# The third block's gates of the second token half also through a table in HBM

## The reference, cut to what matters

```python
s = einsum('thpc,hpkc->thpk', q, sub_keys)         # 8 heads, two halves, 128 keys each
sv, si = top_k(s, 16)
cand = sv[:, :, 0, :, None] + sv[:, :, 1, None, :]  # 16 x 16 pairs of keys
best, pos = top_k(cand, 16)
g = softmax(best)                                   # 8 x 16 = 128 picks of a token
act = gelu(einsum('ted,td->te', u_tab[eidx], x))
y = einsum('te,ted->td', g * act, v_tab[eidx])
```

## Time and profile before

| | us |
|---|---|
| three timed runs | 2058.8, 2061.26, 2061.39; median 2061.26 |
| the profiled execution | 2061.06 |
| its span, first to last instruction | 2059.2 |
| PE busy | 2011.5 (98%) |
| DVE busy | 1544.0 (75%) |
| ACT busy | 959.6 (47%) |
| POOL busy | 784.4 (38%) |
| DMA | 387.68 MB, mean 188 GB/s |

### The profile page before, as it was taken

The page is one execution under the profiler, slowest core; times in us unless marked ns, Lnnn a source line. Parts: engine busy times, 40 slices in busy tenths (PEclk is TensorE's granted clock), DMA queues, the critical chain, the costliest instruction groups (busy, mean ns, idle before and its releaser), DMA issues.

```text
span 2059.2 us, 37564 instructions
## 1 busy us (share of the span) xinstructions
PE 2011.5 (98%) x14922; PEld 1852.2 (90%) x14922; DVE 1544.0 (75%) x2886; ACT 959.6 (47%) x1642; POOL 784.4 (38%) x502
## 2 busy tenths in 40 slices
PE   8999999999999999999998999999999999999998
PEld 7899999999889988887897999999998899888886
DVE  7868996555676578878699879975556766679886
ACT  5654453434444444444655654443434434444443
POOL 1014027777730055642110050088787400456420
PEclk9999999999999999999999999999999999999999
DMA  6684556676765568996422444566667655578973
GB/s 224 211 315 152 168 160 152 156 150 151 183 184 163 178 197 271 329 340 222 133 92 69 128 134 153 174 150 149 157 151 171 182 171 177 190 265 295 326 257 102
DMA packets 165918, 387.68 MB, mean 188 GB/s; under 512 B 55920, under 2 KB 78704, under 8 KB 163440
## 3 DMA queue, kind: packets, MB, share of 16 engines
q1 hardware_dynamic: 113712, 332.58, 49.4%
q0 software_dynamic: 49152, 33.75, 10.4%
q10 hardware_dynamic: 2880, 18.96, 2.3%
HBM read 361.67 MB, written 23.54 MB: 187 GB/s over the span
## 4 chain that ended last, share of the span: by engine, by line
PE 81%; DVE 14%; issue 2%; DMA 2%; ACT 2%; SPq 0%; DVEq 0%; ACTq 0%
PE ps L942 15%; PE ps L944 14%; PE ps L943 14%; PE ps L973 11%; PE ps L975 10%; PE ps L974 10%; PE ps L1020 4%; DVE w_lo L1534 2%; DMA land<-stream_dram 2%; DVE work L1420 2%; ACT w_hi L632 1%; DVE hidden L1420 1%; DVE hidden L1555 0%; DVE hidden L1546 0%; DVE work L1428 0%
## 5 line engine op out<-in xcount | busy, mean ns | idle before, releaser
L1534 DVE TENSOR_TENSOR w_lo<-land,w_hi 128x1024 fp32r<-128x1024 f32 x562 | 686.1, 1221 | 357.1 <-ACT w_hi L632 356.0
L942 PE MATMUL ps<-act_hi,w_hi 128*128 128x288 f32 x2688 | 808.6, 301 | 13.6 <-DVE act_lo L1260 4.8
L632 ACT CAST w_hi<-land 128x1024 fp32r<-128x1024 f32 x592 | 621.5, 1050 | 419.6 <-PE ps L975 299.5
L943 PE MATMUL ps<-act_hi,w_lo 128*128 128x288 f32 x2688 | 795.2, 296 | 0.0
L944 PE MATMUL ps<-act_lo,w_hi 128*128 128x288 f32 x2688 | 792.3, 295 | 0.0
L548 POOL DMA_INDIRECT gates_d<-rstd x256 | 452.6, 1768 | 320.1 <-DVE rstd L1687 193.4
L942 PEld LDWEIGHTS ps<-act_hi,w_hi 128*128 128x128 f32 x2688 | 506.0, 188 | 20.1 <-issue 8.9
L944 PEld LDWEIGHTS ps<-act_lo,w_hi 128*128 128x128 f32 x2688 | 508.1, 189 | 0.0
L943 PEld LDWEIGHTS ps<-act_hi,w_lo 128*128 128x128 f32 x2688 | 507.1, 189 | 1.0
L973 PE MATMUL ps<-w_hi,g_hi 128*128 128x512 f32 x1024 | 403.3, 394 | 5.7 <-DVE g_lo L1839 5.7
L974 PE MATMUL ps<-w_lo,g_hi 128*128 128x512 f32 x1024 | 399.7, 390 | 0.0
(11 more groups left out here) (223 smaller groups left out, 1497.0 us busy)
## 6 DMA issues: line engine op xcount, KB each, us to landing
land<-stream_dram SPq DMA_DIRECT2D x592, 512.0 KB
gates_d<-hidden ACTq DMA_DIRECT2D x16, 1024.0 KB, 5.9
work<-gates_d SPq DMA_DIRECT2D x96, 128.0 KB, 4.5
act_d<-smp_stage SPq DMA_DIRECT2D x64, 64.0 KB
gates_d<-rstd POOLq DMA_INDIRECT x256
hidden<-stream_dram,smp_idx POOLq DMA_INDIRECT x128, 5.9
x<-x_dram SPq DMA_DIRECT2D x4, 288.0 KB, 5.2
y_t_dram<-hidden SPq DMA_DIRECT2D x8, 144.0 KB, 1.9
```

Of the source, the lines that this page charges most:

```text
L632: nc.scalar.copy(w_hi[:, m, :], land[:, n % LANDS, :]).then_inc(w_hi_ready, 1)
L942: nc.tensor.matmul(out, w_hi[:, slot, wsl], hi, start=start, stop=False)
L943: nc.tensor.matmul(out, w_lo[:, slot, wsl], hi, start=False, stop=False)
L1534: V.tensor_tensor(w_lo[:, k, :], land[:, n % LANDS, :], w_hi[:, k, :].bitcast(F32), ALU.subtract).then_inc(lo_by_dve, 1)
```

## The change

The gates of tokens 128 to 255 for tiles 96 to 127 no longer go by one-hots: the 8 chunks of block 2 are dropped (`HOT_BLOCKS = 2`), and a second table per layer takes their place. Of it only the tiles from 96 on are zeroed and read: four more zero fills (two a layer, all four in steps 26 to 32 of layer 0), and 16 more loads of a pair a layer, through four buffers of `gate_land[1]` in the part of `work` that the keys use, in steps 260 to 284. All 128 picks of these tokens are added to the table. POOL's order becomes: heads 0 to 3 of the first table; then, four times, a head of the first and a head of the second; heads 4 and 5 of the second; the act fetches; head 6 of the second; and head 7 of the second in pairs of additions between the row fetches of the first samples. The first table's loads begin in step 192 instead of 180. The samples are added in steps 236 to 285 and summed in step 286. The keys of layer 1 are loaded in step 291 instead of 264, behind the last pair of the second table; the conv state stays in step 264 with a semaphore of its own.

```diff
-GCH = [(TP - t0) // t for t, t0 in zip(GTOK, GTOK0)]
+HOT_BLOCKS = 2
+GCH = [(TP - t0) // t if b < HOT_BLOCKS else 0 for b, (t, t0) in enumerate(zip(GTOK, GTOK0))]
...
-APPLY_AT = [BLOCK_START[1] - 20 + 2 * k for k in range(PAIRS)]
+APPLY_AT = [BLOCK_START[1] - 8 + 2 * k for k in range(PAIRS)]
+SUMMED1 = BLOCKS[2][0]
+PAIRS1 = (P - SUMMED1) // 2
+GATE_LANDS1 = 4
+APPLY1_AT = [min(BLOCK_START[2] - 4 + 2 * k, SLABS - 18 + k - (PAIRS1 - TWICE)) for k in range(PAIRS1)]
...
-ZERO_AT = [3 + 2 * z for z in range(DEPTH * ZERO_N)]
+ZERO1_N = (P - SUMMED1) * P // ZERO_W
+ZERO_AT = [3 + 2 * z for z in range(DEPTH * ZERO_N)] + [Q0 + 2 + 2 * z for z in range(DEPTH * ZERO1_N)]
...
-ADD0, ADD1 = BLOCK_START[1] + 26, SLABS - 12
-ADD_AT = [ADD0 + k * (ADD1 - ADD0) // (SMP - 1) for k in range(SMP)]
-SMP_SUM, SMP_OUT = SLABS - 11, SLABS - 9
+MIXED = 8
+ADD0, ADD1, ADD2 = BLOCK_START[1] + 36, BLOCK_START[1] + 53, SLABS - 11
+ADD_AT = [ADD0 + k * (ADD1 - ADD0) // MIXED for k in range(MIXED)]
+ADD_AT += [ADD1 + k * (ADD2 - ADD1) // (SMP - 1 - MIXED) for k in range(SMP - MIXED)]
+SMP_SUM, SMP_OUT = SLABS - 10, SLABS - 8
...
+                if r - 2 in APPLY1_AT:
+                    k = APPLY1_AT.index(r - 2)
+                    if k == 0:
+                        sp.wait_ge(gate_added[1], 16 * PICKS * (L + 1))
+                        sp.wait_ge(gated, GATES * (L + 1))
+                    if k >= GATE_LANDS1:
+                        sp.wait_ge(pair_gated[1], PAIRS1 * L + k - GATE_LANDS1 + 1)
+                    two = slice(SUMMED1 + 2 * k, SUMMED1 + 2 * k + 2)
+                    sp.dma_start(gate_land[1][:, k % GATE_LANDS1, :],
+                                 gates_d[L][1][:, two, :].rearrange("j i t -> j (i t)")
+                                 ).then_inc(gate_landed[1][k % GATE_LANDS1], 16)
...
+            def add_picks(L, u, picked):
+
+                cells = gates_d[L][u].rearrange("j i (t one) -> (j i t) one", one=1)
+                for k in picked:
+                    if k and k % ADDS == 0:
+                        pool.wait_ge(gate_added[u], 16 * (PICKS * L + k))
+                    nc.gpsimd.indirect_dma_start(
+                        out=cells, out_offset=bass.IndirectOffsetOnAxis(ap=add_idx[u][:, k:k + 1], axis=0),
+                        in_=add_val[u][:, k:k + 1], in_offset=None, compute_op=ALU.add).then_inc(gate_added[u], 16)
+
             def add_gates(L):
...
+                def head(u, h):
+                    add_picks(L, u, range(h * ADDS, h * ADDS + ADDS))
+
+                pool.wait_ge(adds_ready, 2 * L + 1)
+                pool.wait_ge(zeroed, 16 * ZEROS)
+                for h in range(4):
+                    head(0, h)
+                pool.wait_ge(adds_ready, 2 * L + 2)
+                for h in range(4):
+                    head(0, h + 4)
+                    head(1, h)
+                head(1, 4)
+                head(1, 5)
...
+                add_picks(L, 1, range(6 * ADDS, 7 * ADDS))
                 rows = stream.rearrange("s p (two w) -> (s p two) w", two=2)
                 for k in range(SMP):
+                    if 0 < k <= MIXED:
+                        first = 7 * ADDS + 2 * (k - 1)
+                        add_picks(L, 1, range(first, first + 2))
...
                         if e >= SUMMED0:
-                            act.wait_ge(pair_gated, PAIRS * L + (e - SUMMED0) // 2 + 1)
+                            act.wait_ge(pair_gated[0], PAIRS * L + (e - SUMMED0) // 2 + 1)
+                        if e >= SUMMED1:
+                            act.wait_ge(pair_gated[1], PAIRS1 * L + (e - SUMMED1) // 2 + 1)
...
                     if r == BLOCK_START[2] and L == 0:
+                        act.dma_start(cstate, cstate_d).then_inc(cstate_in, 16)
+                    if r == SLABS - 5 and L == 0:
+                        act.wait_ge(pair_gated[1], PAIRS1)
                         act.dma_start(keys, keys_d[1]).then_inc(loaded_l, 16)
-                        act.dma_start(cstate, cstate_d).then_inc(loaded_l, 16)
...
                 soften(L, 0)
-                prepare_adds(L)
+                prepare_adds(L, 0)
                 second_level(L, 2, some_lo)
                 soften(L, 1)
+                prepare_adds(L, 1)
                 soften(L, 2)
...
+                    while paired1 < PAIRS1 and APPLY1_AT[paired1] <= r:
+                        apply_pair(L, paired1, 1)
+                        paired1 += 1
```

More of the change, by code:

```diff
@@ L235, in build @@
         tok_row = sb("tok_row", [P, 1])
-        gates_d = [nc.dram_tensor(f"gates_d{i}", (P, P, P), F32).ap() for i in range(DEPTH)]
+        gates_d = [[nc.dram_tensor(f"gates_d{i}_{u}", (P, P, P), F32).ap() for u in range(2)] for i in range(DEPTH)]
         act_d = [nc.dram_tensor(f"act_d{i}", (P, P, TS), F32).ap() for i in range(DEPTH)]
@@ L405, in build @@
         adds_ready = sem("adds_ready")
-        gate_added = sem("gate_added")
-        gate_landed = [sem(f"gate_landed_{k}") for k in range(GATE_LANDS)]
-        pair_gated = sem("pair_gated")
+        gate_added = [sem("gate_added_0"), sem("gate_added_1")]
+        gate_landed = [[sem(f"gate_landed_{u}_{k}") for k in range((GATE_LANDS, GATE_LANDS1)[u])] for u in range(2)]
+        pair_gated = [sem("pair_gated_0"), sem("pair_gated_1")]
+        cstate_in = sem("cstate_in")
         g_hi_ready = sem("g_hi_ready")
@@ L538, in wide_weights @@
                     nc.gpsimd.tensor_copy(wide_w[:, :, t, t:t + CF_W], taps).then_inc(wide_ready, 1)
-            def add_gates(L):
-                pool.wait_ge(adds_ready, L + 1)
-                pool.wait_ge(zeroed, 16 * DEPTH * ZERO_N)
-                cells = gates_d[L].rearrange("j i (t one) -> (j i t) one", one=1)
-                for k in range(PICKS):
-                    if k and k % ADDS == 0:
-                        pool.wait_ge(gate_added, 16 * (PICKS * L + k))
-                    nc.gpsimd.indirect_dma_start(
-                        out=cells, out_offset=bass.IndirectOffsetOnAxis(ap=add_idx[:, k:k + 1], axis=0),
-                        in_=add_val[:, k:k + 1], in_offset=None, compute_op=ALU.add).then_inc(gate_added, 16)
+            def add_picks(L, u, picked):
[6 more added lines that the diff above has]
+                        in_=add_val[u][:, k:k + 1], in_offset=None, compute_op=ALU.add).then_inc(gate_added[u], 16)
+            def add_gates(L):
+                def head(u, h):
[10 more added lines that the diff above has]
+                head(1, 5)
             def fetch_samples(L):
@@ L636, in zero @@
                 if r in ZERO_AT:
-                    L, z = divmod(ZERO_AT.index(r), ZERO_N)
+                    at = ZERO_AT.index(r)
+                    if at < DEPTH * ZERO_N:
+                        u, (L, z) = 0, divmod(at, ZERO_N)
+                    else:
+                        u, (L, z) = 1, divmod(at - DEPTH * ZERO_N, ZERO1_N)
                     act.wait_ge(zeros_ready, 1)
-                    rows = gates_d[L].rearrange("j i t -> j (i t)")
-                    act.dma_start(rows[:, z * ZERO_W:(z + 1) * ZERO_W], zeros).then_inc(zeroed, 16)
+                    rows = gates_d[L][u].rearrange("j i t -> j (i t)")
+                    lo = u * SUMMED1 * P + z * ZERO_W
+                    act.dma_start(rows[:, lo:lo + ZERO_W], zeros).then_inc(zeroed, 16)
             def square(c, x_count):
@@ L1686, in prepare_adds, with apply_pair @@
+                dve.wait_ge(picks_ready, 3 * L + u + 1)
                 settle()
-                V.tensor_copy(add_val, picks_tok[:, 0, 2, :]).then_inc(adds_ready, 1)
-            def apply_pair(L, k):
-                e, buf = SUMMED0 + 2 * k, k % GATE_LANDS
+                V.tensor_copy(val, picks_tok[:, u, 2, :]).then_inc(adds_ready, 1)
+            def apply_pair(L, k, u):
+                lands, pairs = (GATE_LANDS, GATE_LANDS1)[u], (PAIRS, PAIRS1)[u]
+                e, buf = (SUMMED0, SUMMED1)[u] + 2 * k, k % lands
@@ L1692, in apply_pair @@
                 for half in range(2):
                     dve.wait_ge(evacuated[half], L * USES + USE_U + (e + 2) // 2)
-                dve.wait_ge(gate_landed[buf],
-                            16 * (L * len(range(buf, PAIRS, GATE_LANDS)) + k // GATE_LANDS + 1))
-                two = hidden[:, e % HELD:e % HELD + 2, 0:P]
-                V.tensor_tensor(two, gate_land[:, buf, :].rearrange("p (i t) -> p i t", i=2), two,
-                                ALU.mult).then_inc(pair_gated, 1)
+                dve.wait_ge(gate_landed[u][buf], 16 * (L * len(range(buf, pairs, lands)) + k // lands + 1))
@@ L1700, in add_late @@
+                two = hidden[:, e % HELD:e % HELD + 2, u * P:u * P + P]
+                V.tensor_tensor(two, gate_land[u][:, buf, :].rearrange("p (i t) -> p i t", i=2), two,
+                                ALU.mult).then_inc(pair_gated[u], 1)
             def add_late(L, half):
@@ L1863, in peer @@
                 add_late(L, 0)
-                assert made == applied == GATES and paired == PAIRS
```

(1 more changed line is left out.)

39 lines of the change are left out of this document (21 added, 18 removed).

## The result

The change makes the kernel slower: 2189.54 us, median of five runs (2184.26 to 2192.96), beside 2060.19 (five runs) for the kernel before on the same chip, a ratio of 1.0625 with a 95% interval of 1.061 to 1.064. The forecast was 2131 with a range up to 2165: the side was right, and the size was half, 70 us of 129. The profiled execution took 2187.93 us, 126.9 more than that of before, so its trace can be set against the forecast's sum.

A forecast was written before the change was run, and what follows sets the result against it. TensorE, busy 98% of the span, was taken as the bound. Layers at +35.2 and +35.8 us and small terms at -1 made +70 on 2061.06: 2131 us, forecast range 2105 to 2160, 8-in-10 range 2075 to 2165.

The forecast's parts named there:

- step 194: Where SP asks for the first table; forecast complete at 680 us, asked for at 688.68, so no standstill there.
- The saving: On PE, the third block's 8 expansion chunks a layer vanish, 1.22 us each: 9.8 us a layer won.
- Additions up to 708 us at 2.13: On POOL, one addition with its issue gap takes 2.13 us until block 1's last one-hots end, about 708 us.
- Additions behind 708 us at 1.97: On POOL, one addition with gap takes 1.97 us after block 1's one-hots end, an estimate between 1.84 and 2.13.
- The standstill: PE stands ahead of slab 238 while DVE waits for sample 0: 34.0 us in layer 0, 34.6 in layer 1.
- Samples 1 to 7 at 10 a layer: POOL needs 6.9 us per sample, due every 5.44; DVE waits 1.46 for each of seven; bounds 8 and 15.
- DVE's last stretch at 1 a layer, bounds 0 and 4: Second-table pairs and five more samples fill DVE to 77.5 us against 75.3; slabs in hand cover part: 1 us a layer.
- The keys at -5: Moving the key load away from the conv state in layer 0 wins back 5 us; bounds 0 and 6.3.
- The fills at 3: Four more 1 MB zero fills in layer 0, where DVE waits for the last fill: 3 us lost, between 0 and 13.
- the index at 1 a layer: Second index computation on DVE while PE waits for the first one-hots: 2 us for two layers, 0 to 2.5.
- A: Rival: POOL's additions run at their 1.84 us floor and everything is hidden, giving 2040.5 us; chance 0.10.
- B: Rival: additions at 2.4 us make the first table late too, SP stands 21 us at slab 194, 2231 us; chance 0.06.

The follow-up runs named there:

- the run with four heads: The changed kernel without heads 4 to 7 of the second table (half of its additions) in each layer: 2053.38 us, ratio 0.9957 to the kernel before.
- the thin subtraction: The changed kernel with w_lo of the slabs in steps 200 to 238 computed for 8 of 1024 columns only: 2145.93 us, ratio 1.0406 to the kernel before.

## Why the prediction was wrong

The mechanism was right: the late act fetches, DVE waiting for sample 0 ahead of the next g_lo, PE standing in one place of each layer, then seven smaller waits, and no trouble at step 194. Its sizes weren't.

- **The saving**: 9.8 a layer forecast for eight expansions. The seven in slabs 200 to 236 bring 9.3 and 9.4, and the eighth another 1.2 in slab 240. Right, and rather more.
- **Additions up to 708 us at 2.13**: the 96 between 477.95 and 684.16 have a pitch of 2.15. Right.
- **Additions behind 708 us at 1.97**, "about midpoint of 1.84 and 2.13": the step that failed. In the V steps they take 2.21 and with the gap 2.5 to 2.7, more than anywhere. I took the mean's excess over 1.54 for work that grows less when the one-hots end there. Most of it is w_lo, which every slab has; and where a slab holds little that shifts the beat, one addition after the other meets it. The trace of the kernel before has this already: a held addition ends some 1.42 us behind the end of the DVE instruction that it met. Paired so, 38 of the 57 us that its 256 additions take above 1.54 each belong to w_lo and 15 to the one-hots. The row that said so, the most of 2.55 in the earlier trace rows, I set aside as an exception. The last three heads took 117.5 us for some 103: 22 additions up to slab 200 at a pitch of 2.18, then 26 in V steps at 2.68, one wait for a landing in each part.
- **The standstill**: first rows at 874.65 for 854.5, landed 17.6 us later than forecast, of which 6 are covered because the whole layer is 6.5 late; 45.5 us for 34.0. In layer 1 it is 48.0 for 34.6. DVE's wait has two parts, 13.6 us for the acts and 33.2 for the rows, where one of some 35 was forecast.
- **Samples 1 to 7 at 10 a layer**: 13.5 and 15.1 in the table, but the same slabs are 2.2 and 2.6 us shorter than before in the run with four heads, where no sample is late. So the term is 15.7 and 17.7, above the upper end of 15. That the additions make it is shown by the run without head 7.
- **DVE's last stretch at 1 a layer, bounds 0 and 4**: the second failure, 6.9 and 9.5. I summed DVE's busy times over the whole stretch and took every row as landed. DVE's fullness alone costs 4.1 in layer 1 (four heads); without head 7's additions 2.1 and 4.0 are lost. So some 5 us a layer come from head 7's additions. In layer 1 their way is to be seen: DVE waits four times for a sample's rows, 6.0 us in all. The lines behind this list show two of these waits, PE's standstill behind them, and then 7 us with a granted clock of 0.52, so the lower level (1.2 GHz) for nearly all of it. In layer 0 no such wait stands in this stretch, and how head 7 costs 5 us there stays open.
- **The keys at -5**: 3.5 by the trace and 2.5 by the runs, alone; under the late samples nothing of it is to be seen.
- **The fills at 3, the index at 1 a layer**: 6.5 in layer 0 for both, 0.3 in layer 1 for the index, within their bounds.
- **The range** ended at 2165, since no bound held V steps at 2.5 and none held DVE's stretch above 4.

```profile
2081.40 1.28 DVE L1810 SCALAR_TENSOR_TENSOR hidden<-hidden,smp_act 128x1024 f32<-128x1024 f32 x1 [2.81 <-DMA hidden<-stream_dram,smp_idx]
...
2085.24 1.28 DVE L1810 SCALAR_TENSOR_TENSOR hidden<-hidden,smp_act 128x1024 f32<-128x1024 f32 x1 [0.75 <-DMA hidden<-stream_dram,smp_idx]
2086.44 0.69 DVE L1894 TENSOR_TENSOR g_lo<-hidden,g_hi 128x512 fp32r<-128x512 f32 x1
```

```profile
2087.27 0.76 PE L1021 MATMUL ps<-w_hi,g_hi 128*128 128x512 f32 x1 [3.33 <-DVE g_lo L1894]
```

```profile
2086.00:2093.00 7.00, 5.73 (x14) 4.56 (x15) 5.86 (x8) 0.68 (x2) 5.78 (x5) 0.52 0.94 320
```

Of the rivals, A was refuted, though its ground was real: an addition costs 1.54 where DVE leaves it alone. B didn't come, no wait stands at step 194; additions as dear as its own did, but behind step 200. The Trainium skill, "SBUF — State Buffer", section "Who interferes with whom", has two statements that bear on this. One is that, of DVE in a 2-port mode and GpSimd, whichever gets the shared pair of ports first blocks the other for its whole instruction. For this subtraction the trace shows the like: the addition goes on only when the whole w_lo, or the half that it met, has ended (1.55 to 2.42 us, and 1.72 with halves). The other is that `tensor_tensor` doesn't stall descriptor building, given there as inferred. For the indirect additions here the runs say otherwise: the thin subtraction took them back from 2.42 to 1.55.

## What to carry to other kernels

A free engine's idle time must be priced at what its instructions cost beside the work of the very steps in which they will run, and the most in a view is a candidate for the mean there. Look for a beat: an instruction that waits for another engine's periodic one, with a length near the period, falls into step with it. Before moving work off the bound to an engine with slack, count everything that comes behind it on that engine up to its last due date, not only the part that moves.

## What the hardware showed that was not expected

- An indirect DMA that adds 128 gates takes POOL 1.54 us undisturbed and 1.41 for 64; the fetch of 128 values takes 0.94 to 1.17. A two-input subtraction on DVE over 1024 columns holds it up to 2.42, in two halves the mean there is 1.72. Four quarters, in the U steps, do worse than two halves (1.77 for 1.65): some additions wait for several quarters in a row, and more meet the widest one-hots.
- In the V steps, mostly locked to one a slab, 26 additions took 69.6 us, 2.68 each with the gaps and one wait for a landing; 16 with DVE standing took 29.7, 1.86 each.
- Not every DVE instruction holds an addition up. In the kernel after, 19 additions started beside the product with an input in PSUM (`hidden<-ps,hidden`, 128x512, 0.69 us), and each took 1.54 or 1.55.
- A standstill costs PE more than its length: behind the 45.45 us one, the first products take 0.77 and 0.63 us, where they take 0.39 ahead of it.
